# Part of the down projection's weight sums moved to GpSimd in the up phase, and the accumulators combined on VectorE

## What is computed

```python
h2 = rms_norm(x, norm_mlp_pre)            # 512 x 2048
a = relu(h2 @ w_up)                       # 512 x 8192
x = x + rms_norm((a * a) @ w_down, norm_mlp_post)   # w_down is 8192 x 2048
```

## Time and profile before

| | |
|---|---|
| median of 3 runs | 2442.93 us (2442.41 to 2445.35) |
| the profiled execution | 2442.78 us, span 2441.1 us |
| TensorE busy | 2407.5 us, 99% |
| VectorE, ScalarE, GpSimd busy | 1585.5, 817.4, 507.1 us |
| mean granted TensorE clock | 0.997 |
| moved by DMA | 424.79 MB, mean 174 GB/s |

### The profile page before, as it was taken

How to read it: one execution, slowest core, us unless ns; L and a number is a source line. 1 busy time by engine, 2 the same in 40 slices (tenths; PEclk the granted TensorE clock), 3 DMA queues, 4 the chain that set the end, 5 groups by cost and what they waited for, 6 DMA issues and landing times.

```text
span 2441.1 us, 29976 instructions
## 1 busy us (share of the span) xinstructions
PE 2407.5 (99%) x11506; PEld 1955.5 (80%) x11506; DVE 1585.5 (65%) x1829; ACT 817.4 (33%) x1073; POOL 507.1 (21%) x482
## 2 busy tenths in 40 slices
PE   9999999999999999999999999999999999999988
PEld 7866887878888888888888888888888878777766
DVE  7875688887434442255444444455478888888898
ACT  5145223333422222243222222222245434333333
POOL 1120343431000000002122221222122222222364
PEclk9999999999999999999999999999999999999999
DMA  6431343433334444344557455544568585859453
GB/s 222 118 110 51 104 134 109 126 116 114 129 95 138 144 134 161 100 151 166 192 210 273 166 188 189 193 171 168 195 242 306 199 316 188 321 172 338 152 207 155
DMA packets 97340, 424.79 MB, mean 174 GB/s; under 512 B 19488, under 2 KB 19552, under 8 KB 86720
## 3 DMA queue, kind: packets, MB, share of 16 engines
q1 hardware_dynamic: 65760, 273.71, 33.5%
q0 software_dynamic: 10432, 78.55, 9.1%
q10 hardware_dynamic: 21024, 70.82, 8.1%
HBM read 346.95 MB, written 76.09 MB: 173 GB/s over the span
## 4 chain that ended last, share of the span: by engine, by line
PE 83%; DVE 11%; DMA 3%; issue 2%; ACT 1%; SPq 0%; DVEq 0%; ACTq 0%; POOL 0%
PE main L1897 20%; PE main L1899 20%; PE main L1898 20%; DVE wd_lo L1792 5%; DVE mlp_acc L1801 3%; DMA wd_raw<-wdown 2%; PE side L2215 2%; DVE wd_sums L1785 2%; PE side L2216 2%; PE side L2217 2%; PE main L2215 2%; PE main L2217 2%; PE main L2216 2%; PE side L2117 1%; PE side L2115 1%
## 5 line engine op out<-in xcount | busy, mean ns | idle before, releaser
L1897 PE MATMUL main<-h_hi,w_hi 128*128 128x512 f32 x1792 | 704.3, 393 | 2.2 <-DVE h_lo L1151 1.6
L1899 PE MATMUL main<-h_hi,w_lo 128*128 128x512 f32 x1792 | 697.9, 389 | 0.0
L1898 PE MATMUL main<-h_lo,w_hi 128*128 128x512 f32 x1792 | 697.5, 389 | 0.0
L1135 DVE TENSOR_TENSOR w_lo<-w_raw,w_hi 128x1024 fp32r<-128x1024 f32 x307 | 383.6, 1261 | 267.0 <-ACT w_hi L681 260.3
L681 ACT ACTIVATE w_hi<-w_raw 128x1024 fp32r<-128x1024 f32 x307 | 317.3, 1052 | 439.8 <-PE main L1899 337.0
L1897 PEld LDWEIGHTS main<-h_hi,w_hi 128*128 128x128 f32 x1792 | 336.4, 188 | 77.5 <-issue 5.1
L1899 PEld LDWEIGHTS main<-h_hi,w_lo 128*128 128x128 f32 x1792 | 336.4, 188 | 70.5
L1898 PEld LDWEIGHTS main<-h_lo,w_hi 128*128 128x128 f32 x1792 | 336.6, 188 | 67.9
L632 POOL TENSOR_TENSOR wd_third<-wd_raw 128x512 f32<-128x512 f32 x60 | 130.9, 2183 | 399.1 <-DMA wd_raw<-wdown 268.4
L1792 DVE TENSOR_TENSOR wd_lo<-wd_sums,wd_hi 128x1024 fp32r<-128x1024 f32 x120 | 187.5, 1562 | 33.6 <-ACT wd_hi L1059 33.4
L1059 ACT ACTIVATE wd_hi<-wd_sums 128x1024 fp32r<-128x1024 f32 x120 | 127.5, 1062 | 217.5 <-PE main L2217 90.1
(11 more groups left out here) (363 smaller groups left out, 3862.8 us busy)
## 6 DMA issues: line engine op xcount, KB each, us to landing
w_raw<-wstream SPq DMA_DIRECT2D x307, 512.0 KB, 3.7
wd_raw<-wdown SPq DMA_DIRECT2D x120, 768.0 KB, 5.3
a_scratch<-a_blocks_hi_lo POOLq DMA_DIRECT2D x30, 1792.0 KB, 8.9
a_first_group<-a_scratch ACTq DMA_DIRECT2D x30, 1024.0 KB, 8.8
a_second_group<-a_scratch ACTq DMA_DIRECT2D x28, 768.0 KB, 6.5
gate_scratch<-gate_stage ACTq DMA_DIRECT2D x16, 512.0 KB, 4.0
gate_attn<-gate_scratch POOLq DMA_DIRECT2D x8, 512.0 KB, 3.9
gate_ssm<-gate_scratch POOLq DMA_DIRECT2D x8, 512.0 KB, 4.6
```

Of the source, the lines that this page charges most:

```text
L1135: tt(WL[:, s], RAW[:, s], WH[:, s].bitcast(F32), ALU.subtract).then_inc(lo_ready, 1)
L1897: mm(o, wh, xh[:, k0 + k], start=first and k == 0, stop=False)
L1898: mm(o, wh, xl[:, k0 + k], start=False, stop=False)
L1899: ins = mm(o, wl, xh[:, k0 + k], start=False, stop=last and k == 3)
```

## The change

A list `EARLY` names 24 of the 60 weight pieces (a piece is one pair and one column half, used by one first and one second set): in round 0 three pieces at the beginning, then one or two in rounds 1 to 3, and all twelve of round 4.

- In the up phase GpSimd loads the four raw rows of such a piece (`early_load`, 1024 KB), makes the five combined rows with three operations (`early_sums`: two of 128x1024 and one of 128x512) and stores them to a new DRAM tensor (`early_store`, 1280 KB). One piece is done for each pair k from 1 to 24, between `block_sums(k)` and `store_blocks(k)`.
- In the down phase the 48 sets of these pieces have no `two_sums` on VectorE and no `third_sum` on GpSimd. GpSimd issues loads instead (`load_sums`: 512 KB into `wd_sums`, and for a second set 256 KB into `wd_third`), waiting until the low part of set s-2 is done. SP loads only two raw rows for an early first set and none for an early second one.
- The 16 `combine` operations move from GpSimd to VectorE: 3 in the first three sets of the half's last pass, 5 in the next pass (cb=0) or among the low parts of the plain sets (cb=1).
- The first loads of `a_scratch` by ScalarE's queue move from group 4 to group 14 of the up phase, since their buffers now hold the early pieces; two of the loads that SP issues at the start of the down phase come three loads later.
- The order of the passes, the products, the matmuls and the accumulation stay the same; `PASSES`, `opens`, `closes`, `is_fresh` and `column_of` only write the same order in another way.

```diff
+PASSES = [(r,) + p for r in range(N_ROUND) for p in ((0, True), (0, False), (1, True), (1, False))]
+EARLY = [(0, 0, k) for k in range(3)] + [(r, cb, 3) for r in range(4) for cb in range(2) if r + cb]
+EARLY += [(1, 0, 0), (2, 0, 0)] + [(4, cb, k) for cb in range(2) for k in range(PER)]
...
+    SRAW = [at(f"early_raw{k}", [4, T], kib) for k, kib in enumerate((112, 120))]
+    SSUM = [at(f"early_sums{k}", [5, T], kib) for k, kib in enumerate((128, 138))]
...
+            for n, s in enumerate(raw_sets):
+                if n == 0:
                     sp.wait_ge(lo_ready, N_UNIT - 4)
-                elif s < 3:
-                    sp.wait_ge(lo_ready, N_UNIT - 3 + s)
+                elif n < 3:
+                    sp.wait_ge(lo_ready, N_UNIT - 3 + n)
                 else:
-                    sp.wait_ge(wd_sum, s - 2)
-                    if is_first(s - 3):
-                        sp.wait_ge(wd_lo, 2 * s - 5)
+                    x = raw_sets[n - 3]
+                    if not is_early(x):
+                        sp.wait_ge(wd_sum, summed.index(x) + 1)
+                    if is_first(x):
+                        sp.wait_ge(wd_lo, 2 * x + 1)
                     else:
-                        sp.wait_ge(wd_third, third_of(s - 3) + 1)
-                if s == PER:
+                        sp.wait_ge(wd_third, thirds.index(x) + 1)
+                if n == PER:
                     sp.wait_ge(a_stored, 16 * N_PAIR)
                     sp.wait_ge(unit_done, N_UNIT)
                     for kk in (4, 5):
                         sp.dma_start(AF[kk][:], a_dram[kk][:, 0:4]).then_inc(ax_landed[kk], 16)
+                if n == PER + 3:
+                    for kk in (4, 5):
                         sp.dma_start(AS[kk][:], a_dram[kk][:, 4:7]).then_inc(ay_landed[kk], 16)
-                sp.dma_start(RAWD[s % 3][:], wdown[s // (2 * PER) % 2, s // (4 * PER) * PER + s % PER][:, weights_of(s)]
-                             ).then_inc(wd_landed[s % 3], 16)
+                r, w = slice(1 if is_early(s) else 0, 3), weights_of(s)
+                sp.dma_start(RAWD[n % 3][:, r], wdown[column_of(s), pair_of(s)][:, w.start + r.start:w.stop]
+                             ).then_inc(wd_landed[n % 3], 16)
...
-            def combine(cb, i):
-
-
-                o, y, op = COMBINE[i]
-                x = ACC[:, cb]
-                pool.wait_ge(prod_read, 7 * (2 * N_ROUND - 2 + cb) + (4 if i < 3 else 7))
-                if i:
-                    pool.wait_ge(block_ready, 8 * cb + i)
-                ptt(x[:, o], x[:, o], x[:, y], op).then_inc(block_ready, 1)
...
+            def load_sums(s):
+                u = EARLY.index((PASSES[s // PER][0], column_of(s), s % PER))
+                if s == 1:
+                    pool.wait_ge(lo_ready, N_UNIT)
+                elif s >= 2:
+                    pool.wait_ge(wd_lo, 2 * s - 2)
+                pool.dma_start(TS[s % 2][:], sums_dram[u][:, 0:2] if is_first(s) else sums_dram[u][:, 2:4]
+                               ).then_inc(early_landed[s % 2], 16)
+                if not is_first(s):
+                    n = third_of(s)
+                    if n >= 2:
+                        pool.wait_ge(wd_lo, 2 * seconds[n - 2] + 2)
+                    pool.dma_start(T3[n % 2][:], sums_dram[u][:, 4]).then_inc(early_stored[n % 2], 16)
+            def early_load(n):
+                r, cb, kk = EARLY[n]
+                if n >= 2:
+                    pool.wait_ge(early_ready, n - 1)
+                pool.dma_start(SRAW[n % 2][:], wdown[cb, r * PER + kk]).then_inc(early_landed[n % 2], 16)
+            def early_sums(n):
+                b12, b11, b21, o = SRAW[n % 2][:, 0:1], SRAW[n % 2][:, 1:3], SRAW[n % 2][:, 3:4], SSUM[n % 2]
+                pool.wait_ge(early_landed[n % 2], 16 * (n // 2 + 1))
+                if n >= 2:
+                    pool.wait_ge(early_stored[n % 2], 16 * (n // 2))
+                ptt(o[:, 0:2], b12.to_broadcast([P, 2, T]), b11, ALU.add)
+                ptt(o[:, 2:4], b21.to_broadcast([P, 2, T]), b11, ALU.add)
+                ptt(o[:, 4], SRAW[n % 2][:, 1], SRAW[n % 2][:, 2], ALU.subtract).then_inc(early_ready, 1)
+            def early_store(n):
+                pool.wait_ge(early_ready, n + 1)
+                pool.dma_start(sums_dram[n], SSUM[n % 2][:]).then_inc(early_stored[n % 2], 16)
...
             for k in range(N_PAIR - 2):
                 block_sums(k)
+                if k == 0:
+                    early_load(0)
+                    early_load(1)
+                if 1 <= k <= len(EARLY):
+                    early_sums(k - 1)
+                    early_store(k - 1)
+                    if k + 1 < len(EARLY):
+                        early_load(k + 1)
                 store_blocks(k, 7)
-            for k in range(N_PAIR - 2, N_PAIR):
-                store_blocks(k, 4)
-            for s in range(N_SET):
-                if not is_first(s):
+            store_blocks(N_PAIR - 2, 4)
+            for b in range(2):
+                pool.wait_ge(early_stored[b], 16 * ((len(EARLY) + 1 - b) // 2))
+            load_sums(0)
+            load_sums(1)
+            store_blocks(N_PAIR - 1, 4)
+            for s in range(2, N_SET):
+                if is_early(s):
+                    load_sums(s)
+                elif not is_first(s):
                     third_sum(s)
-                for cb in range(2):
-                    first = N_SET - 3 * PER + 2 * PER * cb
-                    if first + 2 <= s < first + 5:
-                        combine(cb, s - first - 2)
-                    if s == first + 5:
-                        for i in range(3, 8):
-                            combine(cb, i)
             for i in range(4):
...
-                    if h == 4 and j >= 4:
+                    if h == 14 and j == 4:
+                        for b in range(2):
+                            act.wait_ge(early_stored[b], 16 * ((len(EARLY) + 1 - b) // 2))
+                    if h == 14 and j >= 4:
                         load_first(j - 4)
                         load_second(j - 4)
-            two_sums(0)
+            COMBINE = ((S22, S12, ALU.add), (S22, S21, ALU.subtract), (S12, S5, ALU.add), (S22, S11, ALU.add),
+                       (S21, S4, ALU.add), (S11, S4, ALU.add), (S11, S7, ALU.add), (S11, S5, ALU.subtract))
+            def combine(cb, i):
+                o, y, op = COMBINE[i]
+                x = ACC[:, cb]
+                v.wait_ge(prod_read, N_PROD - (7 if cb == 0 else 0) - (3 if i < 3 else 0))
+                if i:
+                    v.wait_ge(block_ready, 8 * cb + i)
+                tt(x[:, o], x[:, o], x[:, y], op).then_inc(block_ready, 1)
+            if not is_early(0):
+                two_sums(0)
             down_lo(0, 0)
-            two_sums(1)
+            if not is_early(1):
+                two_sums(1)
             down_lo(0, 1)
             down_lo(1, 0)
-            two_sums(2)
+            if not is_early(2):
+                two_sums(2)
             up(N_PAIR - 1)
             down_lo(1, 1)
             plain_lo(N_PAIR - 1)
             for s in range(N_SET):
-                if s + 3 < N_SET:
+                if s + 3 < N_SET and not is_early(s + 3):
                     two_sums(s + 3)
-                n = len(products_of(s))
-                for half, js in enumerate((range(0, 2), range(2, n))):
-                    for j in js if s % PER == PER - 1 and s >= 4 * PER else ():
+                n = len(products_of(s)) if closes(s) and not is_fresh(s) else 0
+                for half, js in enumerate((range(0, min(n, 2)), range(2, n))):
+                    for j in js:
                         gather(s, j)
                     down_lo(s + 2, half)
-            down_lo(N_SET + 2, 0)
-            down_lo(N_SET + 2, 1)
-            down_lo(N_SET + 3, 0)
-            down_lo(N_SET + 3, 1)
+                p, kk = s // PER - (len(PASSES) - 4), s % PER
+                if p in (1, 3) and kk < 3:
+                    combine(p // 2, kk)
+                if p == 2 and kk < 5:
+                    combine(0, 3 + kk)
+            for half in range(2):
+                down_lo(N_SET + 2, half)
+            for i in range(3, 8):
+                combine(1, i)
+            for half in range(2):
+                down_lo(N_SET + 3, half)
```

## The result

| | before | after |
|---|---|---|
| median of 6 runs | 2442.73 us (2442.21 to 2445.35) | 2492.83 us (2488.18 to 2499.14) |
| the profiled execution | 2442.78 us, span 2441.1 us | 2493.25 us, span 2491.3 us |
| mean granted TensorE clock | 0.997 | 0.987 |
| first matmul of the down phase starts | 1782.72 | 1837.81 |
| last matmul of the down phase starts | 2431.21 | 2481.76 |

A forecast was written before the change was run, and what follows sets the result against it. The prediction took the down phase's 33.9 us of loss, mostly the last round's GpSimd and VectorE exclusion, as all there was to gain. 2442.8 - 18.0 (down phase) + 23.5 (up phase) = 2448.3 us, range 2420 to 2470.

The forecast's parts named there:

- the stop is of two operations: Up-phase rival: the low part also waits behind GpSimd's third operation, +46, 2471, or 2490 with lost clock; chance 0.16.
- What bounds before: Down phase loses 33.9 us, 20.2 in the last round because GpSimd and VectorE exclude each other; up phase nothing.
- The last round, -19.2: Down phase, last round: its 20.2 us of loss go, but for about 1 us at the gathers of a pass's end.
- The third rival: Round 4's early sets wait for loads, or the start is dearer: +4 to +15; with stores in time, chance 0.12.
- Rounds 1 to 3 [...] their 12.1 us come mostly from gathers and stay: Down phase, rounds 1 to 3: a loss of 12.1 us, mostly from gathers, was to remain unchanged.
- The bound of 8 us a landing: Round 4's second passes: at 8 us per early load, 6 us for each pass, 12 in all; 0 was taken.
- The start, +1.2: Start of the down phase: set 2's load stands behind the last pair's store, costing 1.2 us, between 0 and 4.
- The slack of 5 us for `plain_hi`: Up phase: `plain_hi` may be late by 5 us before TensorE stops.
- The store's landing, T+30.1: Up phase: a pair's store, queued behind early transfers, lands 30.1 us after T, TensorE's start on the unit.
- the scaling from the five loads: Up phase: transfer time scaled from five loads of 5.24 MB in 16.3 us, giving 17.9 us and landing at T+31.2.
- The stop keeps itself: Up phase: a late low part stops TensorE 1.07 us in each of 22 pairs, the same each time, +23.5 us.
- The clock: Clock loss from stops: priced only in the two-operation rival, 2490 with 1 us more a pair.

The follow-up runs named there:

- e4: The kernel before with only the 16 combinations moved to VectorE, at the places of the change, and no early sums: 2431.00 us, ratio 0.9950.
- e7: e5 with the four plain-weight loads (1024 KB each, SP's queue) held back until set 117's first low part is done: 2438.31 us, ratio 0.9979 to before.
- e8: e5 with `a_scratch` loads from pair 6 on cut to a quarter and a third (computation partly wrong): 2419.60 us, ratio 0.9902 to before.
- e2: The changed kernel with only `early_load` moved behind the pair's store, `early_store` staying ahead: 2446.71 us, ratio 1.0010 to before.
- e3: The changed kernel with early sums made and stored but not used, the down phase summing everything itself: 2482.76 us, ratio 1.0155 to before.
- e10: e5 with fewer early pieces: three of round 0, (rounds 1 to 3, cb=1, pair 3), round 4 without four pieces: 2431.37 us, ratio 0.9952 to before.
- e9: The changed kernel with its early additions cut to one of 128x16 from the third piece on (sums wrong), transfers unchanged: 2452.76 us, ratio 1.0040 to before.
- e5: e1 with the first two early loads also moved behind pair 0's store: 2440.66 us, ratio 0.9989 to before.
- e1: The changed kernel with the pair's store issued before `early_store` and `early_load`, additions still in front: 2447.05 us, ratio 1.0011 to before.

## Why the prediction was wrong

It said 2448.3, with a range to 2470; 2492.83 came. The nearest of its cases was "the stop is of two operations" with a lost clock, 2490, at 0.16 with all of that case. Its time is met to 3 us, but by luck: it has 22 stops behind GpSimd's third operation, and there were twelve, behind no operation of GpSimd. Only that a stop costs clock was right in it. By its own steps:

1. *What bounds before*: right. The last round's 20 us came from GpSimd's combinations beside VectorE: e4 took 12 of them by moving these alone.
2. *The last round, -19.2*: -17.0. Passes 16 to 18 went from 15.6 to 0, as stated. Pass 19 kept 4.86. The third rival had early sets wait for their loads, but nothing named what delays these: the plain sets' loads (2409.32) run beside the last early loads (e7, where the slow landing moved with them).
3. *"Rounds 1 to 3 [...] their 12.1 us come mostly from gathers and stay"*: the step that failed in the down phase. TensorE does wait for the gathers, but these stand behind `two_sums`, which wait for raw weights delayed by the blocks' traffic (the rows of before under e8; 3.3 us are left in e8). And they did not stay: they grew by 11.4. The landing of an early load was asked about for round 4 alone, and taken from the median of `w_raw`, 3.7, whose loads are over when the down phase begins, so it knew nothing of the traffic there. Measured, it was 6.3 in the median and up to 7.9 in rounds 1 to 3. The bound of 8 us a landing was right in size; it was put on the wrong rounds.
4. *The start, +1.2*: +0.9.
5. *The slack of 5 us for `plain_hi`*: right; e2 runs 2.0 to 3.5 us late in each pair at no cost, and the stops of after are what lies beyond it.
6. *The store's landing, T+30.1*: T+31.5 in the pair shown, 31.5 to 33.4 in the eleven punctual pairs that come between two stops. The transfer was right and its start wrong: `early_store` was issued at 1557.42, T+14.7 and not T+13.25, and the store landed 16.8 us after that, where the sum had 14.5 + 2.4 = 16.9. Counted from the same issue, the scaling from the five loads (17.9; they were on SP's queue) is 1.1 us too long. The Trainium skill's "DMA: Bandwidth & Descriptors", section "Anatomy of one DMA", from which an estimate of 15.2 us was taken, is 1.6 too short; the other 1.5 us by which its T+28.5 misses are the late issue.
7. *"The stop keeps itself", 22 x 1.07 = 23.5*: the step that failed. First, GpSimd's operations were taken at 2.4 us with one turn of VectorE in every pair; in a pair after a stop, where VectorE is on time, they take 3.39, 2.86 and 2.27, so the bytes start later. Second, the stop was reckoned as VectorE's low part standing behind GpSimd's second operation; in none of the twelve did it stand behind one, and a late `plain_hi` made them alone. Third, a stop is felt back: GpSimd sends its bytes sooner, and the next T comes 4 us later, so the next pair doesn't stop. So there are twelve stops of 2.8 us and not 22 of 1.07: 33.9. Of the 31.6 us missed in the up phase, 10.4 are this.
8. *The clock*: the other 21.2, a term that the sum left out. The text knew of stretches at 1.2 GHz in the last round and gave the clock a price only in its rival. Each of the twelve stops was followed by about 9 matmuls at 0.43 us, 1.8 us on 2.8 of waiting.

Of what would show it: `plain_hi` did wait for `a_scratch`, but started 9.8 to 12.6 us after T in the pairs that stop and on time or nearly in the others; "nothing is short afterwards" did not hold; and a sign named for wrong, stops behind `wd_sums` loads, came in rounds 1 to 3 and in the last pass.

What stays open: how the 11 us that the kernel before loses in rounds 1 to 3 divide between the late raw weights and the gathers themselves; no run takes the blocks' traffic from that kernel. Nor does any run tell why the clock fell behind some stops of the down phase and not behind others.

## What to carry to other kernels

A transfer with a deadline must not be queued behind one without: here three lines in another order were worth 50 us, and with the store first in the queue even additions that compete with VectorE cost nothing. When work is added ahead of a deadline, work out at least two rounds of it, since the second one starts from another state than the first, and price a stop of TensorE above its length (in the up phase here by some 1.8 us). Read the landing time of a new load from loads of the stretch where it will run; a piece that is read back in a stretch full of transfers cost 2 us here where it saved 2.4 of an engine that wasn't the bound.

## What the runs showed of the hardware that was not expected

- A stop's length doesn't tell by itself whether the clock falls behind it. All twelve stops of after's up phase (2.41 to 5.35 us) were followed by 7 to 12 matmuls at 0.43 us. But in the same place of e3, one of 2.43 us was followed by none, and in the down phases stops of 2.93 (e10), 3.27 (e9), 3.58 (e5) and 3.71 us (e8) were followed by none either, while one of 2.46 (e5) was by eight and one of 2.96 (e9) by nine. Stops under 2 us, such as e4's up to 1.91, were followed by none.
- The same 512 KB from DRAM landed in 4.2 us in the median in rounds 1 to 3 of e8 (light block loads), in 6.3 in those of after, and in up to 10.9 beside four loads of 1024 KB. The Trainium skill's "DMA: Bandwidth & Descriptors", section "Queues, rings and completion order", states that each DMA engine takes turns between the queues that it has work for. The runs agree in kind: a small load with little ahead of it in its own queue came late while others were busy.
- The order in a queue alone, with the same bytes in it, moved the store's landing from 12.2 to 6.3 us and that of `early_load` from 10.1 to 14.3 (e1): the time is passed on to the transfer that can bear it.
